# First adaLN chunk of a two-layer decoder trunk in two halves of the channels

## Chip, cores and metric

The kernel runs on one core of a Trainium2 chip. The metric is device microseconds (us) of one execution. Engines are called as the profile calls them: PE (TensorE matmul), PEld (its weight load), DVE (VectorE), ACT (ScalarE), POOL (GpSimd), SP (SyncE, which here only issues loads). A trailing q (SPq) is an engine's sequencer.

## What is computed

Two layers over 256 tokens of 1024 channels, float32. Cut to what the change touches:

```python
c_act = silu(c)
for l in range(2):
    mod = c_act @ w_ada[l] + b_ada[l]                     # 1024 x 6144
    shift1, scale1, gate1, shift2, scale2, gate2 = split(mod, 6)
    h = rmsnorm(x, norm1_g[l]) * (1.0 + scale1) + shift1
    u = h @ w_in[l]                                       # 1024 x 3072
    u_b, u_c, u_h, u_q, u_k, u_v = split(u, 6 blocks of 512)
    y_conv = u_b * conv3(u_c * u_h)
    q, k = rope(rmsnorm(heads(u_q))), rope(rmsnorm(heads(u_k)))
    y_att = causal attention of 8 heads of 64 (q, k, v)
    x = x + gate1 * (concat(rmsnorm(y_conv), rmsnorm(y_att)) @ w_out[l])
    x = x + gate2 * hier_moe(rmsnorm(x, norm2_g[l]) * (1.0 + scale2) + shift2)
```

To have u, every one of the 1024 channels of h is needed; h needs shift1 and scale1 of the same channels, and each value of these sums over all 1024 rows of w_ada.

## The kernel before

**Loads.** SP issues one stream of 1 MB units into `raw`, a ring of ten slots of 128 x 2048 floats: first 8 "a" units (w_ada of layer 0, columns 0 to 2047, that is shift1 and scale1), then 12 "w" units of w_in (each 512 of the 1024 rows by one block of 512 columns, blocks in the order q, k, v, then the three of the convolution), then the chunk of the gates ("G", 8 units), w_out, and so on. An "a" unit k holds, in partition p, row 8p + k of w_ada as one piece of 8 KB; a "w" unit holds pieces of 2 KB. SP waits for a slot to be free (`wait_free`) and goes on in order. x, small parameter rows and the gate biases come by ACT's queue, router weights by POOL's.

**adaLN (lines 1088 to 1112, 442 to 448, 753 to 765).** `ada_acc` multiplies each "a" unit by silu(c), repeated over 32 columns: four matmuls a unit write four strips of 32 rows of PSUM bank 6, 512 columns each. They are float32, and the profile records each as two. `ada_out` (ACT) copies the bank to `mod_rows`, `ada_cols` (PE, four matmuls against `rowsel`) turns the rows into columns, `modulation` (DVE) adds the bias and makes the factor.

**Activations.** PE transposes the normed x into banks 0 to 3 (`transposes`), ACT scales and shifts two channel blocks of 128 a bank into `hf` (`norm_evac`, L470), and DVE splits them into a high and a low part (L783, L784), one part for each bank, four in all. act_ready counts them.

**Weights.** Each w unit is two halves of 1024 columns. ACT copies a half rounded into `whi` (L435), DVE subtracts into `wlo` (L694); both are rings of six halves. A product takes three matmuls (`PASSES`).

**q, k, v (L1178).** Block by block: q over all 8 channel blocks into banks 4 and 5, then k into 0 and 1, then v into 2 and 3; 48 matmuls of 512 columns each, 144 in all. Then `conv_block` 0, 1, 2 (L1190, 96 matmuls of 256 columns each), with the transposes of q and k (L1203) between 1 and 2, for which DVE must have done squares, reduction (L805, L807) and rope (L812 to L828).

Every engine works through its own list in order. In layer 0 ACT has: ada_out, norm_evac of four banks, halves 0 to 5, then halves 6 on between the evacuations. DVE has: modulation, four activation parts, halves 0 to 5, the eight trig products (L795), halves 6 to 11, squares and so on. PE has: three "a" units, transposes of parameter rows (L1152, L1155), three "a" units, transposes of x, two "a" units, ada_cols, then q, k, v.

## Time and profile before

| | us |
|---|---|
| median of 3 runs (lowest, highest) | 659.57 (655.09, 663.69) |
| profiled execution, its own time | 659.15 |
| its span, first to last instruction | 657.4 |
| PE busy, matmuls | 578.3 (88%) |
| DVE busy | 281.8 (43%) |
| ACT busy | 217.5 (33%) |
| moved by DMA | 189.76 MB, mean 289 GB/s |

The profile is of one execution; the runs scatter by about 0.7% round their median. Matmuls are pipelined and their ends modelled, so their starts are the surer reading. The clock column has no record before about 28 us, where it prints 1.00; there durations are read instead.

### The profile page before, as it was taken

What the parts mean: (1) busy time and instruction counts of PE and PEld (TensorE: products, weight loads), DVE (VectorE), ACT (ScalarE), POOL (GpSimd) and SP (SyncE); (2) the same over time, 40 slices, a digit from 0 to 9 for tenths busy, and PEclk for the clock granted to TensorE, in tenths of its full rate; (3) what the DMA queues carried; (4) which work ended last, traced back from release to release, by engine and by line L of the source; (5) the groups of instructions that cost most, each with busy time, mean ns of one, the idle gap of its engine ahead of it and who ended that gap; (6) DMA issues with size and microseconds to landing.
All of it is one profiled execution on the core that took longest, in us unless ns stands there. A gap on an engine that the chain in (4) does not pass through costs nothing.

```text
span 657.4 us, 7967 instructions
## 1 busy us (share of the span) xinstructions
PE 578.3 (88%) x3204; PEld 371.1 (56%) x3204; DVE 281.8 (43%) x483; ACT 217.5 (33%) x376; POOL 13.2 (2%) x63
## 2 busy tenths in 40 slices
PE   2759999869799999999948999986977899999993
PEld 0338899446666644444427899754566664444432
DVE  4065790875256111112277595476236401111233
ACT  2064543541134322322135535254105332322210
POOL 6100000000000000000000000000000000000000
PEclk9959999989898799999998999987977679999998
DMA  8999942790399799999999545195058059999951
GB/s 266 371 390 387 376 171 110 286 413 4 135 420 410 274 378 396 413 412 415 406 386 362 201 168 216 65 415 224 1 227 349 0 186 372 409 414 415 414 220 66
DMA packets 48623, 189.76 MB, mean 289 GB/s; under 512 B 4346, under 2 KB 4426, under 8 KB 40388
## 3 DMA queue, kind: packets, MB, share of 16 engines
q1 hardware_dynamic: 47264, 185.62, 72.3%
q10 hardware_dynamic: 900, 3.23, 1.3%
q0 software_dynamic: 416, 0.32, 0.6%
q8 instruction: 29, 0.48, 0.3%
q14 instruction: 14, 0.11, 0.0%
HBM read 188.10 MB, written 1.05 MB: 288 GB/s over the span
## 4 chain that ended last, share of the span: by engine, by line
PE 79%; DVE 9%; DMA 4%; ACT 4%; issue 1%; SPq 1%; DVEq 0%; ACTq 0%
PE ps L1370 18%; PE ps L1190 11%; PE ps L1178 10%; PE ps L1396 9%; PE ps L1350 6%; PE ps L1281 6%; PE ps L1098 5%; PE ps L1410 4%; DMA raw<-in_w_ada_dram 4%; DVE wlo L694 2%; PE ps L1322 2%; PE ps L1121 2%; PE ps L1436 1%; PE ps L1111 1%; PE ps L1271 1%
## 5 line engine op out<-in xcount | busy, mean ns | idle before, releaser
L694 DVE TENSOR_TENSOR wlo<-raw,whi 128x1024 fp32r<-128x1024 f32 x64 | 74.9, 1220 | 14.4 <-ACT whi L435 14.2
L435 ACT ACTIVATE whi<-raw 128x1024 fp32r<-128x1024 f32 x64 | 64.6, 1061 | 26.3 <-PE ps L1178 10.9
L1098 PE MATMUL ps<-raw,c_rep 128*32 128x512 f32 x384 | 53.5, 696 | 17.2 <-DMA raw<-in_w_ada_dram 17.2
L1370 PE MATMUL ps<-raw,qkT 128*64 128x512 f32 x256 | 61.5, 625 | 1.9 <-ACT work L645 1.9
L1396 PE MATMUL ps<-raw,work 128*64 128x512 f32 x256 | 58.0, 598 | 0.0
L1370 PE MATMUL ps<-raw,cbc 128*64 128x512 f32 x256 | 57.2, 594 | 0.0
L1190 PE MATMUL ps<-act_hi,whi 128*128 128x256 f32 x192 | 54.5, 284 | 0.0
L1190 PE MATMUL ps<-act_hi,wlo 128*128 128x256 f32 x192 | 54.3, 283 | 0.0
L1190 PE MATMUL ps<-act_lo,whi 128*128 128x256 f32 x192 | 54.3, 283 | 0.0
L1045 DVE SCALAR_TENSOR_TENSOR work<-ps,cw,work 128x256 f32<-128x256 f32 x16 | 7.7, 483 | 108.1 <-ACT work L639 108.1
L1034 DVE TENSOR_TENSOR v_sb<-ps,gates 128x512 f32<-128x512 f32 x32 | 22.1, 691 | 67.2 <-PE ps L1396 67.2
L1178 PE MATMUL ps<-whi,act_hi 128*128 128x512 f32 x96 | 38.6, 402 | 8.7 <-DVE wlo L694 7.1
L1098 PEld LDWEIGHTS ps<-raw,c_rep 128*32 128x32 f32 x384 | 11.7, 120 | 48.3 <-issue 33.9
L1370 PEld LDWEIGHTS ps<-raw,qkT 128*64 128x64 f32 x256 | 18.1, 143 | 36.0 <-issue 31.5
L1178 PE MATMUL ps<-wlo,act_hi 128*128 128x512 f32 x96 | 38.2, 397 | 0.0
L1178 PE MATMUL ps<-whi,act_lo 128*128 128x512 f32 x96 | 38.1, 396 | 0.0
L1370 PEld LDWEIGHTS ps<-raw,cbc 128*64 128x64 f32 x256 | 18.0, 137 | 34.8 <-issue 33.7
L629 ACT ACTIVATE whi<-v_sb 128x512 fp32r<-128x512 f32 x32 | 20.0, 630 | 53.5 <-DVE v_sb L1034 45.2
L1350 PE MATMUL ps<-whi,act_hi 128*128 128x256 f32 x128 | 37.0, 320 | 0.3 <-DVE whi L990 0.3
L1190 PEld LDWEIGHTS ps<-act_hi,wlo 128*128 128x128 f32 x192 | 36.8, 192 | 0.1
L1190 PEld LDWEIGHTS ps<-act_hi,whi 128*128 128x128 f32 x192 | 36.8, 192 | 0.1
L1190 PEld LDWEIGHTS ps<-act_lo,whi 128*128 128x128 f32 x192 | 36.8, 192 | 0.0
(207 smaller groups left out, 886.7 us busy)
## 6 DMA issues: line engine op xcount, KB each, us to landing
raw<-in_w_ada_dram SPq DMA_DIRECT2D x48, 1024.0 KB, 9.7
raw<-in_w_gate_dram SPq DMA_DIRECT2D x64, 512.0 KB, 7.3
raw<-in_w_up_dram SPq DMA_DIRECT2D x64, 512.0 KB, 9.4
raw<-in_w_down_dram SPq DMA_DIRECT2D x32, 1024.0 KB, 11.5
raw<-in_w_in_dram SPq DMA_DIRECT2D x24, 1024.0 KB, 14.5
raw<-in_w_out_dram SPq DMA_DIRECT2D x8, 1024.0 KB, 6.1
gates<-in_b_ada_dram ACTq DMA_DIRECT2D x4, 512.0 KB, 6.8
res<-in_x_dram ACTq DMA_DIRECT2D x1, 1024.0 KB, 4.9
```

The costliest lines, as they stand in the source:

```text
L435: act.activation(whi[:, slot(n), :], raw[:, r, (i % 2) * 1024:(i % 2 + 1) * 1024], ACT.Copy).then_inc(hi_done, 1)
L629: act.activation(y_hi[:, cols], y_f[:, cols], ACT.Copy).then_inc(yhi_ready, 1)
L694: dve.tensor_tensor(wlo[:, slot(n), :], raw[:, ring_slot[("w", l, i // 2)], (i % 2) * 1024:(i % 2 + 1) * 1024], whi[:, slot(n), :].bitcast ...
L1034: dve.tensor_tensor(y_f[:, cols], ps[:, 2 + n, :], gates[:, 1, cols], ALU.mult).then_inc(yg_ready, 1)
L1098: ins = pe.matmul(ps[32 * i:32 * i + 32, 6, :], c_rep[:, k, :], raw[:, ring_slot[unit], i * 512:(i + 1) * 512], start=(k == 0), stop=(k == ...
L1178: ins = pe.matmul(ps[:, bank + t, :], acts[pa][:, k, t * P:(t + 1) * P], w[pw][:, kk * 512:(kk + 1) * 512], start=(k == 0 and p == 0), sto ...
L1190: ins = pe.matmul(ps[:, bank + j // 2, (j % 2) * S:(j % 2 + 1) * S], w[pw][:, kk * 512 + j * P:kk * 512 + (j + 1) * P], acts[pa][:, k, :], ...
L1281: ins = pe.matmul(ps[:, 2 * t + n, :], acts[pa][:, k, t * P:(t + 1) * P], w[pw][:, n * 512:(n + 1) * 512], start=(k == 0 and p == 0), stop ...
L1350: ins = pe.matmul(ps[:, bank, j * S:(j + 1) * S], xn[part][:, t, k * P:(k + 1) * P], sel[:, t, 256 * q:256 * (q + 1)], start=(t == 0 and p ...
L1370: ins = pe.matmul(ps[i * SLOTS:(i + 1) * SLOTS, 0, :], hg[p // 2 % 2][:, k, c0:c0 + SLOTS], ws[i][:, :, kk, :], start=(k == 0), stop=(k == ...
L1396: ins = pe.matmul(ps[i * SLOTS:(i + 1) * SLOTS, 2 + n, :], hidT[:, p % 2, kk, i * SLOTS:(i + 1) * SLOTS], ws[i][:, c0:c0 + 512], start=(kk ...
L1410: ins = pe.matmul(ps[:, 4 + 2 * t + n, :], selT[:, 2 * p + t, :], ys[part][:, n * 512:(n + 1) * 512], start=(p == 0 and part == 0), stop=( ...
```

## The change

The first chunk is made in two: A0 gives shift1 and scale1 of channels 0 to 511, A1 those of 512 to 1023. An "a" unit of these holds two rows of w_ada (8p + 2i and 8p + 2i + 1) with 512 + 512 columns of each, in two DMAs of 512 KB in pieces of 2 KB; A0 and A1 have four units each. The stream becomes A0, the first w units of q, k and v (channels 0 to 511), A1, the rest. Turning rows into columns (`first_cols`) still takes four matmuls, each time.

PE now has: two A0 units, transposes of parameter rows, transposes of x, two A0 units, first_cols(0), q on channels 0 to 511, one A1 unit, k on these, two A1 units, v on these, one A1 unit, first_cols(1), then q, k and v on channels 512 to 1023. ACT copies the transposes of channels 512 to 1023 out of PSUM unscaled (so that v can use banks 2 and 3) and scales them in place later. DVE has: first_modulation(0), two activation parts, halves 0 to 5, first_modulation(1), two activation parts, the trig products, halves 6 on. The order q, k, v by halves of the channels holds for both layers, and the evacuations of q, k and v and DVE's halves 12 to 23 are moved accordingly. The lines left out are declarations and renumbered semaphore counts.

```diff
@@ -242,19 +244,26 @@
-        chunks = [("A", 0)]
+        chunks = [("A0", 0), ("A1", 0)]
         for l in range(L):
             chunks += [("G", l), ("M", l)] + ([("A", l + 1)] if l + 1 < L else [])
         chunk_of = {q: i for i, q in enumerate(chunks)}
         steps_before = [sum(2 if kind == "G" else 1 for kind, _ in chunks[:i]) for i in range(len(chunks))]
+        chunk_units = [4 if kind in ("A0", "A1") else KD for kind, _ in chunks]
+        units_before = [sum(chunk_units[:i]) for i in range(len(chunks) + 1)]
+
+        def in_unit(u):
+
+            return (IN_ORDER[u % 3], u // 3) if u < 6 else (IN_ORDER[u // 2], u % 2)
         def slot(n):
             return (n + 1) % RING
-        stream = [("a", 0, k) for k in range(KD)]
+        stream = [("a", 0, k) for k in range(4)] + [("w", 0, u) for u in range(3)]
+        stream += [("a", 1, k) for k in range(4)]
         for l in range(L):
-            stream += [("w", l, u) for u in range(0 if l == 0 else 2, 12)]
+            stream += [("w", l, u) for u in range(3 if l == 0 else 2, 12)]
             stream += [("a", chunk_of[("G", l)], k) for k in range(KD)]
@@ -291,6 +300,13 @@
                     row = ada_v[layer, :, i, :]
+                    if which in ("A0", "A1"):
+                        c0 = 512 * int(which == "A1")
+                        for j in range(2):
+                            sp.dma_start(dst.rearrange("p (j v n) -> p j v n", j=2, v=2)[:, j, :, :],
+                                         ada_v[layer, :, 2 * i + j, 0:2 * D].rearrange("p (v n) -> p v n", v=2)
+                                         [:, :, c0:c0 + 512]).then_inc(raw_full[r], 16)
+                        return
                     if which == "G":
@@ -482,15 +498,28 @@
                 root(0, t)
-            ada_out("A", 0)
-            norm_evac(0, range(4))
+            for bank in (2, 3):
+                act.wait_ge(xT_done, bank + 1)
+                ins = act.activation(hf[:, 2 * bank:2 * bank + 2, :],
+                                     ps[:, bank, :].rearrange("p (j s) -> p j s", j=2), ACT.Copy)
+            ins.then_inc(hf_raw, 1)
+            ada_out("A0", 0)
+            norm_evac(0, range(2))
+            split(0, 0)
+            split(0, 1)
+            split(0, 2)
+            ada_out("A1", 0)
+            act.wait_ge(mod_ready, 2)
+            act.wait_ge(hf_raw, 1)
+            for bank in (2, 3):
+                for j in (2 * bank, 2 * bank + 1):
+                    ins = act.activation(hf[:, j, :], hf[:, j, :], ACT.Identity, scale=mod_t[:, 0, 1, j:j + 1],
+                                         bias=mod_t[:, 0, 0, j:j + 1])
+                ins.then_inc(hf_act, 1)
             for l in range(L):
                 n0 = HALVES * l
                 m = 2 * l
-                if l == 0:
-                    for u in range(3):
-                        split(l, u)
-                else:
+                if l > 0:
                     for t in range(T):
@@ -500,25 +529,25 @@
                 def qk_out(w):
-                    act.wait_ge(unit_used, n0 + 4 * (w + 1))
+                    act.wait_ge(unit_used, n0 + 8 + 2 * w)
                     bank = (4, 0)[w]
                     for t in range(T):
                         ins = act.activation(tokmaj[:, t, w * AW:(w + 1) * AW], ps[:, bank + t, :],
                                              ACT.Copy)
                     ins.then_inc(proj_evac, 1)
-                qk_out(0)
                 split(l, 4)
                 split(l, 5)
+                qk_out(0)
+                split(l, 6)
                 qk_out(1)
-                split(l, 6)
                 split(l, 7)
+                act.wait_ge(unit_used, n0 + 12)
+                act.activation(v_sb[:, :, :], ps[:, 2:4, :], ACT.Copy).then_inc(proj_evac, 1)
+                split(l, 8)
                 act.wait_ge(qk_sum, l + 1)
                 act.activation(stat[:, 4:36], stat[:, 4:36], ACT.Sqrt, scale=1.0 / HD,
                                bias=eps_col).then_inc(qk_root, 1)
-                act.wait_ge(unit_used, n0 + 12)
-                act.activation(v_sb[:, :, :], ps[:, 2:4, :], ACT.Copy).then_inc(proj_evac, 1)
-                split(l, 8)
                 split(l, 9)
@@ -750,6 +781,17 @@
+            def first_modulation(a):
+
+                dve.wait_ge(mod_sum, a + 1)
+                ks = slice(4 * a, 4 * a + 4)
+                dve.tensor_tensor(mod_t[:, 0, :, ks], ps[:, 7, 0:8].rearrange("p (j v) -> p v j", v=2),
+                                  mod_col[:, 0, ks, 0:2].rearrange("p j v -> p v j"), ALU.add).then_inc(mod_read, 1)
+                dve.wait_ge(mod_read, a + 1)
+                dve.scalar_tensor_tensor(out=mod_t[:, 0, 1, ks], in0=mod_t[:, 0, 1, ks], scalar=1.0,
+                                         in1=mod_col[:, 0, ks, 6 * L], op0=ALU.add, op1=ALU.mult
+                                         ).then_inc(mod_ready, 1)
+
             def modulation(kind, l):
@@ -771,20 +813,29 @@
-            modulation("A", 0)
+            def activation_parts(l, banks):
+                for bank in banks:
+                    dve.wait_ge(hf_act, 6 * l + bank + 1)
+                    js = slice(2 * bank, 2 * bank + 2)
+                    link(dve.tensor_copy(act_hi[:, js, :], hf[:, js, :]))
+                    dve.tensor_tensor(act_lo[:, js, :], hf[:, js, :], act_hi[:, js, :].bitcast(F32),
+                                      ALU.subtract).then_inc(act_ready, 1)
+
+            first_modulation(0)
+            activation_parts(0, range(2))
+            for u in range(3):
+                split(0, u)
+            first_modulation(1)
+            activation_parts(0, range(2, 4))
             for l in range(L):
                 n0 = HALVES * l
                 if l > 0:
                     for t in range(T):
                         token_scale(2 * l, t)
-                for bank in range(4):
-                    dve.wait_ge(hf_act, 6 * l + bank + 1)
-                    js = slice(2 * bank, 2 * bank + 2)
-                    link(dve.tensor_copy(act_hi[:, js, :], hf[:, js, :]))
-                    dve.tensor_tensor(act_lo[:, js, :], hf[:, js, :], act_hi[:, js, :].bitcast(F32),
-                                      ALU.subtract).then_inc(act_ready, 1)
-                for i in range(0 if l == 0 else 3, 6):
-                    split_half(l, i)
+                if l > 0:
+                    activation_parts(l, range(4))
+                    for i in range(3, 6):
+                        split_half(l, i)
                 if l == 0:
@@ -799,6 +850,7 @@
                 split(l, 5)
+                split(l, 6)
@@ -806,8 +858,8 @@
                                   AX.X, ALU.add).then_inc(qk_sum, 1)
-                split(l, 6)
                 split(l, 7)
+                split(l, 8)
                 dve.wait_ge(qk_root, l + 1)
@@ -828,8 +880,7 @@
                     dve.wait_ge(rope_done, T * l + t + 1)
-                    split(l, 8 + t)
-                split(l, 10)
+                    split(l, 9 + t)
                 split(l, 11)
@@ -1095,10 +1146,21 @@
                     for i in range(4):
-                        ins = pe.matmul(ps[32 * i:32 * i + 32, 6, :], c_rep[:, k, :],
+                        row = 2 * k + i // 2 if q < 2 else k
+                        ins = pe.matmul(ps[32 * i:32 * i + 32, 6, :], c_rep[:, row, :],
                                         raw[:, ring_slot[unit], i * 512:(i + 1) * 512],
-                                        start=(k == 0), stop=(k == KD - 1), skip_group_check=True)
+                                        start=(k == 0), stop=(k == chunk_units[q] - 1), skip_group_check=True)
                     ins.then_inc(ada_used, 1)
+
+            def first_cols(a):
+
+                pe.wait_ge(mod_evac, a + 1)
+                if a > 0:
+                    pe.wait_ge(mod_read, a)
+                for j in range(4):
+                    ins = pe.matmul(ps[:, 7, 2 * j:2 * j + 2], mod_rows[:, j * P:(j + 1) * P], rowsel2[:, :],
+                                    start=True, stop=True)
+                ins.then_inc(mod_sum, 1)
@@ -1141,7 +1203,7 @@
             pe.wait_ge(crep_ready, 2)
-            ada_acc("A", 0, range(0, 3))
+            ada_acc("A0", 0, range(0, 2))
             pe.wait_ge(const_ready, 2)
@@ -1155,30 +1217,42 @@
             ins.then_inc(lines_T, 1)
-            ada_acc("A", 0, range(3, 6))
             transposes(0)
-            ada_acc("A", 0, range(6, 8))
-            ada_cols("A", 0)
+            ada_acc("A0", 0, range(2, 4))
+            first_cols(0)
             for l in range(L):
                 n0 = HALVES * l
                 if l > 0:
                     transposes(2 * l)
-                for i in range(3):
+                for u in range(6):
+                    i, part = u % 3, u // 3
                     bank = (4, 0, 2)[i]
-                    if i > 0 and l == 0:
-                        pass
-                    for half in range(4):
-                        w = wait_half(l, 4 * i + half)
-                        pe.wait_ge(act_ready, 4 * l + (4 if i else half + 1))
+                    if l == 0 and i == 2 and part == 0:
+                        pe.wait_ge(hf_raw, 1)
+                    elif i == 2 and part == 0:
+                        pe.wait_ge(act_ready, 4 * l + 4)
+                    for half in range(2):
+                        w = wait_half(l, 2 * u + half)
+                        if i == 0:
+                            pe.wait_ge(act_ready, 4 * l + 2 * part + half + 1)
+                        elif i == 1 and part == 0 and half == 0:
+                            pe.wait_ge(act_ready, 4 * l + 2)
                         for kk in range(2):
-                            k = 2 * half + kk
+                            k = 4 * part + 2 * half + kk
                             for t in range(T):
                                 for p, (pa, pw) in enumerate(PASSES):
                                     ins = pe.matmul(ps[:, bank + t, :], acts[pa][:, k, t * P:(t + 1) * P],
                                                     w[pw][:, kk * 512:(kk + 1) * 512],
                                                     start=(k == 0 and p == 0), stop=(k == KD - 1 and p == 2))
                         ins.then_inc(unit_used, 1)
+                    if l == 0 and u == 0:
+                        ada_acc("A1", 0, range(0, 1))
+                    elif l == 0 and u == 1:
+                        ada_acc("A1", 0, range(1, 3))
+                    elif l == 0 and u == 2:
+                        ada_acc("A1", 0, range(3, 4))
+                        first_cols(1)
...
```

## Rows read from the trace of the kernel before

**Rows 1.** Page: PE's busy tenths in 40 slices; split of weights on ACT, mean ns.

```profile
PE   2759999869799999999948999986977899999993
...
L435 ACT ACTIVATE whi<-raw 128x1024 fp32r<-128x1024 f32 x64 | 64.6, 1061 | 26.3 <-PE ps L1178 10.9
```

**Rows 2.** Chain of waits, 0 to 125 us: start us, us, what.

```profile
5.02 27.93 DMA raw<-in_w_ada_dram
...
43.75 35.06 PE ps L1178 x144
...
101.88 1.03 ACT cbc L529
```

**Rows 3.** SP's loads into raw, fourth w_ada unit and third w_in unit: duration ns, start.

```profile
L299 SPq DMA_DIRECT2D raw<-in_w_ada_dram x1: 447/447/447, 2.9 to 2.9; - x1
...
DMA to landing us min/median/max: 19.0/19.0/19.0
...
L302 SPq DMA_DIRECT2D raw<-in_w_in_dram x1: 10356/10356/10356, 19.1 to 19.1; - x1
...
DMA to landing us min/median/max: 21.9/21.9/21.9
```

**Rows 4.** Timeline of PE, 0 to 44 us: start us, us, operation, count, idle before.

```profile
15.07 1.94 PE L1098 MATMUL ps<-raw,c_rep 128*32 128x512 f32 x8 [2.81 <-DMA raw<-in_w_ada_dram]
...
20.97 1.97 PE L1152 MATMUL ps<-ident,cbc 16*128 16x16 f32 x16
...
23.29 3.64 PE L1098 MATMUL ps<-raw,c_rep 128*32 128x512 f32 x16
...
28.63 1.97 PE L1130 MATMUL ps<-ident,tokmaj 128*128 128x128 f32 x16
30.52 1.07 PE L1098 MATMUL ps<-raw,c_rep 128*32 128x512 f32 x8
...
34.77 1.87 PE L1111 MATMUL ps<-rowsel,mod_rows 128*128 128x4 f32 x8 [0.72 <-ACT mod_rows L448]
```

**Rows 5.** Timeline of DVE, 36 to 50 us: modulation, first activation part, six weight splits.

```profile
36.95 0.17 DVE L763 SCALAR_TENSOR_TENSOR mod_t<-mod_t,mod_col 128x8 f32<-128x8 f32 x1
38.22 0.43 DVE L783 CAST act_hi<-work 128x512 fp32r<-128x512 f32 x1 [1.09 <-ACT work L470]
...
42.47 6.89 DVE L694 TENSOR_TENSOR wlo<-raw,whi 128x1024 fp32r<-128x1024 f32 x6
```

**Rows 6.** Chain of waits, later: the same forms at full rate.

```profile
125.80 3.57 PE ps L1098 x32
...
206.06 0.88 PE ps L1111 x8
...
350.80 32.90 PE ps L1178 x144
```

**Rows 7.** Timeline of DVE, 49 to 86 us: trig products to the first rope.

```profile
49.29 1.16 DVE L795 TENSOR_TENSOR trig<-sincos,g_qk 128x64 f32<-128x64 f32 x8
...
69.08 2.48 DVE L805 TENSOR_TENSOR work<-tokmaj 128x1024 f32<-128x1024 f32 x2 [4.18 <-ACT tokmaj L506]
71.60 2.29 DVE L807 TENSOR_REDUCE stat<-work 128x32 f32<-128x2048 f32 x1
...
78.34 0.35 DVE L812 RECIPROCAL stat<-stat 128x32 f32<-128x32 f32 x1
...
83.85 2.36 DVE L694 TENSOR_TENSOR wlo<-raw,whi 128x1024 fp32r<-128x1024 f32 x2
```

**Rows 8.** Windows: us, busy PE, PEld, DVE, ACT, POOL, granted clock, DMA share, GB/s.

```profile
40.00:45.00 5.00, 1.25 (x3) 1.06 (x4) 4.93 (x8) 5.00 (x8) 0.00 (x0) 0.50 1.05 388
...
120.00:125.00 5.00, 2.55 (x23) 1.24 (x16) 4.79 (x9) 3.85 (x17) 0.00 (x0) 1.00 0.99 376
```

**Rows 9.** DMA, 270 to 330 us (expert stage), and landings of loads, 75 to 95 us.

```profile
DMA packets 6132, 24.61 MB, mean 410 GB/s; under 512 B 566, under 2 KB 566, under 8 KB 5009
...
DMA to landing us min/median/max: 4.9/5.9/6.0
```

More of the change, by code:

```diff
@@ L93, in trunk @@
         rowsel = sb("rowsel", [P, 4])
+        rowsel2 = sb("rowsel2", [P, 2])
         mask = sb("mask", [P, 384])
@@ L170, in trunk @@
         xT_done = sem("xT_done")
+        hf_raw = sem("hf_raw")
         hf_act = sem("hf_act")
@@ L276, in trunk @@
             r = pos % RAW
-            counts[r] += 32 if unit[0] == "g" else 16
+            counts[r] += 32 if unit[0] == "g" or unit[0] == "a" and unit[1] < 2 else 16
             ring_slot[unit], landed[unit] = r, counts[r]
@@ L300, in load @@
                 elif kind == "w" and i < 12:
-                    blk, half = IN_ORDER[i // 2], i % 2
+                    blk, half = in_unit(i)
                     sp.dma_start(dst.rearrange("p (k n) -> p k n", k=4),
@@ L321, in wait_free @@
                 if kind == "a":
-                    sp.wait_ge(ada_used, KD * l + i + 1)
+                    sp.wait_ge(ada_used, units_before[l] + i + 1)
                 elif kind == "w":
@@ L444, in ada_out @@
                 q = chunk_of[(kind, l)]
-                act.wait_ge(ada_used, KD * (q + 1))
+                act.wait_ge(ada_used, units_before[q + 1])
                 if q > 0:
@@ L464, in norm_evac @@
             def norm_evac(m, banks):
-                act.wait_ge(mod_ready, m + 1)
+                act.wait_ge(mod_ready, m + 2 if m > 0 else 1)
                 for bank in banks:
@@ L716, in _ @@
             dve.memset(stat[:, 63:64], EPS).then_inc(crep_ready, 1)
+            dve.memset(rowsel2[:, :], 0.0)
             link(dve.memset(rowsel[:, :], 0.0))
             for i in range(4):
+                dve.memset(rowsel2[32 * i:32 * i + 1, i % 2:i % 2 + 1], 1.0)
                 last = dve.memset(rowsel[32 * i:32 * i + 1, i:i + 1], 1.0)
@@ L943, in _ @@
                 dve.reciprocal(stat[:, 1:2], stat[:, 3:4]).then_inc(rstd_ready, 1)
-                dve.wait_ge(mod_ready, m + 1)
+                dve.wait_ge(mod_ready, m + 2)
                 for bank in (2, 3):
@@ L1423, in _ @@
                 if l + 1 < L:
-                    pe.wait_ge(mod_ready, m + 2)
+                    pe.wait_ge(mod_ready, m + 3)
                 pe.wait_ge(over_known, l + 1)
```

## The prediction, made before the changed kernel was timed

> **What bounds the kernel now.** I read the page first, its line of PE's busy tenths: nearly all digits are 7 to 9, but the first two are 2 and 7 [rows 1]. The start is where PE is not yet the bound. The chain of waits says what is instead: 27.93 us of it are one landing of adaLN weights, issued at 5.02 and there at 32.95, and from 43.75 PE works without a gap to 101.9, where an evacuation comes in [rows 2]. The question is therefore how early the q, k, v matmuls (L1178) can end; they end at 43.75 + 35.06 = 78.81, and what follows is a PE chain that starts from there.
>
> Landings next. Issue time plus time to landing gives for the fourth megabyte of the chunk 2.9 + 19.0 = 21.9 us and for the third of w_in, the eleventh in the stream, 19.1 + 21.9 = 41.0 [rows 3]; the eighth has 32.95. That is one megabyte in 2.7 us from the fourth to the eighth, whose pieces have 8 KB, and in 2.7 us from there to the eleventh, whose pieces have 2 KB.
>
> The path between the last landing and the first matmul is read off the timelines. PE accumulates the eighth unit in 1.1 us from 32.95, ACT evacuates, PE turns the rows into columns from 34.77 on [rows 4], and DVE is done with the modulation at 37.12 [rows 5]. ACT and DVE then evacuate and split the activations, four parts of 1.06 us on DVE (38.22 to 42.47), DVE splits the first weights (6.89 / 6 = 1.15 us each) [rows 5], and PE starts at 43.75.
>
> **The start of the first half, costed.** After the change PE needs only four units (4 MB, landed at 21.9). Its queue: unit 1 ends at 17.0 (15.07 + 1.94), the small transposes of the parameter rows take 20.97 to 23.29 = 2.3, transposes(0) 28.63 to 30.52 = 1.9, units 2 and 3 at 1.94 each [rows 4]: 17.0 + 2.3 + 1.9 + 3.9 = 25.1. By then all of it has landed, so PE, not the DMA, ends the first half. ACT's raw evacuation of banks 2 and 3 comes before the new ada_out; it can begin at 21.2 and copies 128x1024 in all, about 1.0 us by L529 [rows 2], done before 25.1, so it costs nothing. From the end of the accumulation to mod_ready was 34.1 to 37.12 = 3.0; first_cols still issues four matmuls (eight records), so it stays 3.0: 28.1. From mod_ready to the first matmul was 6.6; two of the four activation parts (2 x 1.06 = 2.1) leave the path: 4.5. PE starts at **32.6 instead of 43.75: -11.1**. Bounds: with units 2, 3 and the columns at the faster rate that the same forms show later (1.07 a unit at 30.52, 0.88 for the columns at 206 [rows 4, 6]) it is 29.9; if the parameter rows land only at 20.97, which the trace does not exclude, 36.6.
>
> **What comes onto PE.** The A1 units used to be accumulated while PE had nothing else. Now they stand between the q, k and v parts. They have landed by then (32.95 to 41.0, the places of the old eighth to eleventh megabyte), so each costs only its work, 3.57 / 4 = 0.89 us at full rate [rows 6]: **+3.6**. The matmuls themselves keep their number, 144, and their slow beginning: the same 144 take 32.90 in layer 1, at full rate throughout [rows 6], and 35.06 here, 2.2 more. u0, u1, u2 with the four units between them take 16.45 + 2.2 + 3.6 = 22.2 us and end at 54.8.
>
> **The new bubble.** The fourth A1 unit ends at 54.8, almost fourteen us after it landed, and nothing that PE could do stands behind it. In order: evacuation 0.7, columns 0.88 at full rate [rows 6], modulation 0.4: mod_ready at 56.8 (2.0 together). Then ACT scales the first bank, 37.16 to 38.22 = 1.06 before, now out of SBUF; the nearest rows, 128x1024 from SBUF in 1.06 and from PSUM in 1.02, say that the source changes little [rows 1, 2]. DVE splits two activation parts (2.1). And then, ahead of the first wlo of w3, DVE has the eight trig products of L795: in the kernel before they ran at 49.29 for 1.16 us under PE's work [rows 7]; here they stand alone, 1.2. Last one wlo, 1.2. 1.06 + 2.1 + 1.2 + 1.2 = 5.6. ACT's halves 6 and 7 are ready in that time; its two gate bias DMAs are issued by its sequencer while ACT works. **Bubble 2.0 + 5.6 = +7.6**; PE restarts at 62.4.
>
> **The restart.** After the gap of 7.1 us before 43.75 the granted clock was 0.50 (1.2 of 2.4 GHz) [rows 8]. Against it, from 120 to 125 PE was busy for 2.55 of 5 us and kept 1.00 [rows 8]. Here PE has two gaps, 0.7 and 5.6 us, round 0.88 of columns; that is nearer to the first row, so I take the same price again: **+2.2**, bounds 0 and 3. The Trainium skill (TensorE: Matmul & The Clock Gate, HAM oscillation) says that an idle gap puts the array back to half rate and each restart pays anew, which speaks against splitting one long run into two; by it the sum is the one below, without it 2.2 less.
>
> **Sum.** -11.1 + 3.6 + 7.6 + 2.2 = **+2.3 us** at the end of v: 81.1 instead of 78.8.
>
> **What I cost at nothing.** (a) The later q and k. All three blocks now end in the last half of the section, so DVE's squares, reduction and rope start later in both layers: k is out at 77 instead of 69. Squares and reduction take 4.8, a pair of wlo 2.4, one rope 78.34 to 83.85 = 5.5 [rows 7]. A conv block takes 11.5 us (78.81 to 101.88 for two), so its second unit is wanted 5.8 after its start. From k out, DVE has unit 7 ready at 76.7 + 4.8 + 2.4 = 83.9, wanted at 81.1 + 5.8 = 86.9; then unit 8, a rope and unit 9 by 94.2, wanted at 98.4; the second rope (5.1) by 99.3, wanted by the transposes at 105.2. The old slack was about 11 us (the second rope ended some 7.5 after 83.85, the transposes began at 102.9). If the cover were gone, each us of lateness beyond 3 would show in each layer. (b) Sixteen transfers of 512 KB for eight of 1 MB: SP issues one in about 0.45 us [rows 3], and the stream needs 1.35 us for 512 KB. In the expert stage, where gate and up come in transfers of 512 KB, the stream keeps 410 GB/s [rows 9]. (c) The gate biases (1 MB) are loaded 15 us later; they are wanted far behind, by the gates after the attention. (d) SP's ring: w6 to w11 wait for slots that first-half units free earlier than before, and units 8 MB ahead are not on the path. (e) Layer 1: same units in the same number, 32.90 us together, with act_ready asked no earlier than before. (f) The memsets of rowsel2 run on DVE while it waits for positions and x.
>
> **Rivals.** *The change does what it says:* the second half's modulation is hidden, the bubble and the second slow start vanish, and -11.1 + 3.6 = -7.5 remains: 651.6 us. For it: A1 has landed at 41.0. Against it: first_cols(1) follows the last accumulation directly, and the splits of w3 stand behind it on ACT and DVE. An earlier start at 29.9 or no slow restart alone gives 657 to 659. Chance of the whole or most of it 0.08.
>
> *The split transfers come late.* In a quiet queue a 1 MB transfer takes 4.9 us to land [rows 9] against 2.7 in the stream, so 2.2 us of it are fixed. If the four extra DMAs of A0 each paid that, A0 lands at 30.7; unit 3 ends at 32.6, 7.5 us later than I have it, and the time is 669.0. A1 would land at 58.6, still before PE wants its last unit. The stream's rate in the expert stage speaks against it. Chance 0.07. The Trainium skill (DMA: Bandwidth & Descriptors, Bandwidth) asks for at least 1 MiB a DMA and gives one as 2.0 us plus bytes / 436 GB/s; an estimate by that page, were the eight of 512 KB run one after another, is 26 us for A0, and the trace at 410 GB/s does not bear it out.
>
> *Slower, by DVE.* Between k out and the second rope DVE is on the path. It decides when DVE's work there (22 us: squares to second rope) runs more than 3 us later than summed; at 9.6 us late, 6.6 show in each of two layers, and the time is 661.5 + 13.2 = 675. The durations come from rows, so it would need another wait there, such as ACT's square root standing behind v's evacuation. Chance 0.04.
>
> **Numbers.** The forecast has 0.81. Against the profiled execution's own time of 659.15 (span 657.4 plus 1.75) the sum gives 661.5; that execution is 0.4 below the median of the runs. The bounds give 656.6 (PE starts at 29.9 and restarts at full rate, -2.7 and -2.2) to 666.3 (late parameter rows and a restart of 3, +4.8), and the rivals 651.6, 669.0 and 675; with less than two in ten left out, and two or three us for the spread of the runs, the range is 653.5 to 667.5. Two per cent, about what a measurement of this kernel can tell from no change, is 13.2 us: only below 646.4 or above 672.8. Even the first rival in full does not reach that on the fast side. Faster 0.03, within 0.92, slower 0.05.
>
> **What the new profile would show.** First L1178 near 32.6 (not before 30) and A0's last unit done near 25; the first half's q, k, v ending with the fourth A1 unit near 55; a PE gap of about 5.6 us before the second half, its last releaser DVE's wlo, with the trig products just before it; half rate after it; L1190 starting near 81; no wait of L1190 or L1203 on DVE. I am wrong if the second gap is much shorter, if A0 lands after 25, or if PE waits in conv blocks 0 or 1.

## The result, and the profile after

| | before | after |
|---|---|---|
| median (lowest to highest), us | 659.48 (655.09 to 663.69), 4 executions | 669.48 (668.46 to 670.33), 4 executions |
| ratio, 95% interval | | 1.0152 (1.0084 to 1.0220) |
| profiled execution, span | 657.4 | 666.7 |
| its mean granted clock | 0.929 | 0.912 |

The changed kernel is 10 us, 1.5%, slower; the forecast was 661.5, in a range up to 667.5. Ratios in this document leave out executions more than 1.5% above the fastest of their kernel; medians count all.

First the start of the changed kernel. The chain of waits, start us, us, what; L1150 accumulates adaLN units, L1161 makes columns, L1245 is q, k, v, L1264 the conv blocks:

```profile
3.17 12.37 DMA raw<-in_w_ada_dram
...
26.17 1.07 PE ps L1161 x8
...
32.19 8.15 PE ps L1245 x24
40.34 0.99 PE ps L1150 x8
41.34 5.67 PE ps L1245 x24
47.01 1.85 PE ps L1150 x16
48.86 5.71 PE ps L1245 x24
54.57 1.04 PE ps L1150 x8
55.63 0.61 ACT mod_rows L464
...
56.28 1.07 PE ps L1161 x8
...
63.51 18.77 PE ps L1245 x72
82.28 23.05 PE ps L1264 x192
```

The landing that was 27.93 us of the chain [rows 2] is now 12.37, and q starts at 32.19 instead of 43.75. But the first halves of q, k and v with the A1 units between them last until 55.6, the second half starts only at 63.51, and the section ends at 82.28 against 78.81: **+3.5 us** where all of the gain was to be.

The gap from 57.35 to 63.51 is DVE's list, and its timeline shows it whole (start us, us, operation):

```profile
57.57 0.17 DVE L791 SCALAR_TENSOR_TENSOR mod_t<-mod_t,mod_col 128x4 f32<-128x4 f32 x1
58.90 0.43 DVE L820 CAST act_hi<-work 128x512 fp32r<-128x512 f32 x1 [1.16 <-ACT work L516]
59.36 0.69 DVE L821 TENSOR_TENSOR act_lo<-work,act_hi 128x512 fp32r<-128x512 f32 x1
...
61.03 1.17 DVE L846 TENSOR_TENSOR trig<-sincos,g_qk 128x64 f32<-128x64 f32 x8
62.23 6.90 DVE L723 TENSOR_TENSOR wlo<-raw,whi 128x1024 fp32r<-128x1024 f32 x6
```

Modulation, a wait for ACT's scaling, two activation parts, the trig products that had lain under PE's work [rows 7], one weight split.

The section is a third of the loss. The windows, cut at the same instructions in both kernels, tell where the rest is (us of the stretch, busy time and count of PE, PEld, DVE, ACT, POOL, granted clock, DMA share, GB/s). Before:

```profile
104.05:158.62 54.57, 46.60 (x345) 30.39 (x344) 33.75 (x59) 21.81 (x49) 0.00 (x0) 0.94 0.53 212
158.62:345.95 187.33, 172.74 (x880) 95.19 (x881) 59.72 (x117) 54.91 (x99) 0.00 (x0) 0.94 0.90 357
345.95:383.70 37.75, 36.17 (x162) 30.33 (x163) 26.17 (x36) 18.80 (x26) 0.00 (x0) 0.96 0.70 247
408.94:466.84 57.90, 49.93 (x346) 31.22 (x344) 34.41 (x60) 21.93 (x49) 0.00 (x0) 0.88 0.51 200
466.84:657.40 190.56, 169.08 (x808) 98.10 (x808) 52.12 (x103) 49.60 (x92) 0.00 (x0) 0.91 0.67 265
```

After, the same five:

```profile
107.53:165.72 58.19, 50.21 (x345) 32.13 (x344) 34.43 (x60) 21.81 (x49) 0.00 (x0) 0.85 0.53 212
165.72:352.57 186.85, 172.23 (x880) 94.98 (x880) 59.09 (x115) 54.84 (x99) 0.00 (x0) 0.94 0.90 358
352.57:392.31 39.74, 38.56 (x162) 32.04 (x163) 23.40 (x32) 18.90 (x25) 0.00 (x0) 0.89 0.70 249
417.55:476.22 58.67, 50.32 (x345) 32.12 (x344) 34.42 (x60) 21.81 (x49) 0.00 (x0) 0.85 0.52 210
476.22:666.70 190.48, 169.15 (x809) 98.18 (x808) 52.16 (x103) 49.55 (x92) 0.00 (x0) 0.91 0.66 265
```

The same instructions (345, 880, 162), yet the attention of layer 0 takes 58.19 instead of 54.57 us (+3.6), the start of layer 1 39.74 instead of 37.75 (+2.0), layer 1's attention +0.8; the rest is within 0.5. Wherever time was lost the granted clock is lower: 0.85 against 0.94, 0.89 against 0.96, 0.85 against 0.88. It is not longer waiting: in layer 0's attention PE is idle for 7.97 us before and 7.98 after, and all that was lost is in its busy time (50.21 against 46.60). With 3.5 of the section the sum is 3.5 + 3.6 - 0.5 + 2.0 + 0.8 - 0.1 = 9.3, the difference of the spans. So 5.8 us were lost behind the section, at half rate. The attention is code that the change left as it was. In the start of layer 1 the change did alter the order of q, k, v, but that is not what costs the 2.0 us: this stretch took 39.77 in a profile with the old order (e6) and 37.74 in two with the new one (e8, e11). None of my terms covered the 5.8 us.

Inside layer 0's attention the chains show where it happens. Before:

```profile
139.32 1.14 DVE gates L772
140.45 0.14 issue
140.59 3.58 PE ps L1121 x4
...
146.67 3.22 PE ps L1271 x8
...
151.62 7.00 PE ps L1098 x64
```

After:

```profile
142.81 1.14 DVE gates L814
143.95 0.14 issue
144.08 3.75 PE ps L1183 x4
...
150.96 3.78 PE ps L1345 x8
...
157.19 8.53 PE ps L1150 x64
```

In both kernels PE waits 3.7 us for DVE's gates ahead of the first of these matmuls, and in both the granted clock goes to 0.50 towards the end of that wait. Before, it stood there from about 140.4 to 143.9 and again from 147.3 to 150.7; after, from about 143.2 to 160.3 without a break. The wait is the same; what differs is when full rate comes back. The start of layer 1 has the same picture behind a wait of 7.8 us: full rate is back at 348.7, ahead of q, k, v (350.8), in the kernel before, and at 361.6, four us into them, in the changed one.

### The profile page after: what moved, and what is told of

It is laid out like the page before. It is cut to its first block, busy times and chain, and to the rows that moved or that the text cites. A ratio compares the mean times of both kernels' runs of the same rounds, so it can differ in the third digit from the quotient of the medians.

```text
span 666.7 us, 7993 instructions
## 1 busy us (share of the span) xinstructions
PE 586.5 (88%) x3212; PEld 378.5 (57%) x3212; DVE 282.4 (42%) x490; ACT 218.8 (33%) x379; POOL 13.2 (2%) x63
## 4 chain that ended last, share of the span: by engine, by line
PE 81%; DVE 10%; ACT 4%; DMA 2%; issue 1%; DVEq 0%; SPq 0%; ACTq 0%
PE ps L1444 17%; PE ps L1245 11%; PE ps L1264 10%; PE ps L1470 9%; PE ps L1424 6%; PE ps L1355 6%; PE ps L1150 6%; PE ps L1484 4%; DVE wlo L723 2%; DMA raw<-in_w_ada_dram 2%; PE ps L1183 2%; PE ps L1396 2%; PE ps L1192 1%; PE ps L1510 1%; PE ps L1345 1%
## 5 line engine op out<-in xcount | busy, mean ns | idle before, releaser
L1150 PE MATMUL ps<-raw,c_rep 128*32 128x512 f32 x384 | 50.9, 670 | 13.7 <-DMA raw<-in_w_ada_dram 13.7
L1264 PE MATMUL ps<-act_hi,whi 128*128 128x256 f32 x192 | 54.5, 284 | 0.0
L1264 PE MATMUL ps<-act_hi,wlo 128*128 128x256 f32 x192 | 54.3, 283 | 0.0
L1264 PE MATMUL ps<-act_lo,whi 128*128 128x256 f32 x192 | 54.3, 283 | 0.0
L1245 PE MATMUL ps<-whi,act_hi 128*128 128x512 f32 x96 | 40.8, 425 | 12.3 <-DVE wlo L723 11.1
L1245 PE MATMUL ps<-wlo,act_hi 128*128 128x512 f32 x96 | 39.9, 416 | 0.0
L1245 PE MATMUL ps<-whi,act_lo 128*128 128x512 f32 x96 | 39.7, 414 | 0.0
L1264 PEld LDWEIGHTS ps<-act_hi,wlo 128*128 128x128 f32 x192 | 36.8, 192 | 0.1
L1264 PEld LDWEIGHTS ps<-act_hi,whi 128*128 128x128 f32 x192 | 36.8, 192 | 0.1
L1264 PEld LDWEIGHTS ps<-act_lo,whi 128*128 128x128 f32 x192 | 36.8, 192 | 0.0
L1424 PEld LDWEIGHTS ps<-whi,act_hi 128*128 128x128 f32 x128 | 26.4, 206 | 18.2 <-issue 18.2
```

The costliest lines, as they stand in the source:

```text
L1150: ins = pe.matmul(ps[32 * i:32 * i + 32, 6, :], c_rep[:, row, :], raw[:, ring_slot[unit], i * 512:(i + 1) * 512], start=(k == 0), stop=(k ...
L1245: ins = pe.matmul(ps[:, bank + t, :], acts[pa][:, k, t * P:(t + 1) * P], w[pw][:, kk * 512:(kk + 1) * 512], start=(k == 0 and p == 0), sto ...
L1264: ins = pe.matmul(ps[:, bank + j // 2, (j % 2) * S:(j % 2 + 1) * S], w[pw][:, kk * 512 + j * P:kk * 512 + (j + 1) * P], acts[pa][:, k, :], ...
L1424: ins = pe.matmul(ps[:, bank, j * S:(j + 1) * S], xn[part][:, t, k * P:(k + 1) * P], sel[:, t, 256 * q:256 * (q + 1)], start=(t == 0 and p ...
```

## The experiments

The question after the result: do those 5.8 us come anew in each execution by chance (A), do they come with a later schedule (B), or do they depend on where the section ends against the changes of the clock (C)? And are the terms of the section what I said?

**The kernel before again (e1).** No edit.

> The kernel before once more, to see the stretch from 119 us on in a second profiled execution. Theory A (the 5.9 us that the changed kernel loses behind the q, k, v matmuls come from where the stretches of half rate fall, and these fall anew in each execution): the spans scatter by some 5 us and a new profile shows other stretches of half rate than 140.4 to 143.9 and 147.3 to 150.7. Theory B (they come with the schedule): the same stretches again within 1 us, span 655 to 660.

Median 656.84 (654.96 to 659.85) in 10 executions, ratio 0.9988 (0.9953 to 1.0023). The profiled one has span 654.0 and clock 0.936, and layer 1's attention took 53.7 us there against 57.9 in the first profile. So half rate does fall differently from one execution to the next. Layer 0's attention was as before, though (54.65 us, with half rate in the same two stretches), so theory B had this part right. The kernel before has a spread of 9 us: over 31 executions of that chip 654.4, at a clock of 0.936, to 663.4, at 0.921.

**The new order of q, k, v alone (e2).** On the kernel before:

```diff
-                    blk, half = IN_ORDER[i // 2], i % 2
+                    blk, half = in_unit(i)
-                for i in range(3):
+                for u in range(6):
+                    i, part = u % 3, u // 3
```

with the evacuations and DVE's splits moved as in the change.

> The kernel before with one part of the change alone: q, k, v by halves of the channels in both layers, with the evacuations and the splits moved as in the change; the first chunk stays whole. My prediction's point (a) costs this at nothing: 657 to 662 us, the first q, k, v matmul at 43.7, the last ending at 78.8, no wait in the conv blocks. The rival (DVE late behind k) would show a wait of L1190's counterpart or of the transposes of q and k on DVE and 2 us or more in each layer.

Median 659.97 (655.25 to 661.08), ratio 1.0030 (1.0002 to 1.0057). In its chain the conv blocks follow q, k, v without a wait (43.95 + 35.67, then 23.05 us for 192 matmuls as before), and no DVE piece stands between. Point (a) holds: DVE's later work is covered. Layer 0's attention took 56.3 us here and the start of layer 1 39.7, at a lower clock than before; the 0.3% are within what half rate moves.

**Trig products early (e3, again in e15).** On the changed kernel, DVE:

```diff
             for u in range(3):
                 split(0, u)
+            trig_products(0)
             first_modulation(1)
             activation_parts(0, range(2, 4))
```

> The changed kernel with the eight trig products of layer 0 moved ahead of first_modulation(1), into time in which DVE waits. If the gap of 6.2 us before the second half is the chain modulation, scaling, two activation parts, trig products, one weight split, it shrinks by 1.2 to 5.0 us and the last q, k, v matmul ends at 81.1 instead of 82.3. If something else held PE there (ACT's halves 6 and 7), nothing moves. The total follows by 1.2 us, or by more or less if the stretches of half rate fall otherwise.

PE's gap fell from 6.18 to 5.04 us and the second half started at 61.96: the term is right. But the whole kernel came to 660.68 (658.48 to 663.03), ratio 1.0056 (1.0030 to 1.0081): 1.2 us of work moved off the path, some 8 us gained. None of its ten executions had a clock below 0.924.

**A1 behind the first part of q (e4, e8, e16).** On the changed kernel, PE:

```diff
+                        if l == 0 and u == 1 and half == 0:
+                            first_cols(1)
                     if l == 0 and u == 0:
-                        ada_acc("A1", 0, range(0, 1))
-                    elif l == 0 and u == 1:
-                        ada_acc("A1", 0, range(1, 3))
-                    elif l == 0 and u == 2:
-                        ada_acc("A1", 0, range(3, 4))
-                        first_cols(1)
+                        ada_acc("A1", 0, range(0, 4))
```

> The changed kernel with all four A1 units accumulated directly behind the first part of q and first_cols(1) in the middle of the first part of k, so that the second modulation lies under the rest of k and v. If the bubble is an order of work and not a late landing, PE runs without a gap from 32.2 to the end of v: 82.3 - 7.9 (bubble) - 2.3 (half rate after it) + 1.0 (columns) = 73 us, some 6 us ahead of the kernel before; the whole kernel 653 to 661 us. If A1 lands later than the 41 us of my sum, PE waits in the A1 units instead and the end lies later by that wait.

q, k, v started at 33.41 and ended at 73.81 with no gap: the four A1 units took 3.64 us at 41.79, the columns 0.95 at 48.22. So the bubble was the order of PE's list, not a landing, and the whole of it can be hidden. The kernel as a whole: 658.23 (651.73 to 660.50), ratio 0.9991 (0.9954 to 1.0028). Its ten executions fall apart by clock: three at 651.7 to 653.7 with 0.933 to 0.934, four at 658.8 to 660.5 with 0.916, and three at 655.1 to 659.0 between. The 5 us are won in the section and mostly lost again behind it: in the profiled execution (660.41) the two attentions took 58.2 and 58.7 us.

**The changed kernel again (e5, e13).** No edit.

> The changed kernel once more, in many executions. The q, k, v section accounts for +3.5 us. Theory A (the other 5.9 us are half rate that falls anew in each execution): the executions scatter over 5 us or more, as those of the kernel before and of e4 did (654 to 663, 652 to 660), with a median of 657.6 + 3.5 = 661 us. Theory B (the shifted schedule keeps PE at half rate behind it in every execution): again 668 to 670 with a granted clock of 0.909 to 0.912 in all.

668.57 (664.63 to 670.35) in 5 executions, ratio 1.0148 (1.0098 to 1.0199); one had 0.924 and 664.63, four had 0.912. With the first four and e13's five, 13 of 14 executions on several chips lie at 0.909 to 0.912. Theory A falls: chance would not miss so evenly.

The exception is the execution that was profiled here, and it tells more than the rest. Its section ended at 84.61, 2.3 us later than in the first profile, and its two attentions took 54.35 and 54.78 us instead of 58.19 and 58.67, at 0.94 instead of 0.85. With no line of code changed, a later end of the section went with 3.8 us less in all (664.63 against 668.46).

**The kernel before, delayed (e6).** DVE, ahead of the first weight split of layer 0:

```diff
+                if l == 0:
+                    for _ in range(8):
+                        link(dve.memset(trig[:, :, :, :, :], 0.0))
```

> The kernel before with eight fills of an unused tile, each waited for, on DVE ahead of its first weight split: the q, k, v matmuls start about 3.5 us later (3 to 5), nothing else differs, and they end about where those of the changed kernel do. Theory A: the median moves by the delay alone, to some 661 us. Theory B (a shift of that size is enough to bring the half rate behind it): 666 to 670 us.

The fills took 0.66 us each, 5.1 together, more than expected; q, k, v started at 47.90 and ended at 82.44, where the changed kernel's end. The median is 664.48 (659.45 to 668.62) against 659.77, ratio 1.0078 (1.0039 to 1.0116): +4.7 us for a section that ends 3.6 later, between the forecasts of both theories. In the median a shift costs about what it is, and the changed kernel with the same end of the section is 4 us slower; so a shift alone does not bring the whole loss. But it brings part of it: in the profiled execution (665.80) layer 0's attention took 58.27 us and the start of layer 1 39.77, as in the changed kernel, while layer 1's attention took 54.51. So these two losses do not need the changed kernel's code.

**The gap filled (e7).** On the changed kernel, PE, behind first_cols(1):

```diff
+                        for _ in range(12):
+                            pe.matmul(ps[0:32, 6, :], c_rep[:, 0, :], tokmaj[:, 0, 0:512],
+                                      start=True, stop=True)
```

> The changed kernel with twelve further matmuls (32 x 512, float32, results thrown away, into a bank that is free) behind first_cols(1), in the gap before the second half. If the second slow start is the answer to PE's idleness, the 72 matmuls after it take 16.5 instead of 18.8 us and the section ends 2.3 us earlier; if half rate comes there anyway, nothing moves. The twelve should take 5.1 us of the 6.2.

The chain of this kernel:

```profile
57.13 10.42 PE ps L1257 x24
67.54 16.54 PE ps L1245 x72
84.09 23.05 PE ps L1267 x192
```

The twelve took 10.4 us, twice what I gave them (0.87 each: only a group of four, on four strips, is done in 0.89), so the second half started 4.0 us later and the section ended at 84.09. But the half ran in 16.54 us, at a clock of 1.00, instead of 18.77: the second slow start is PE's idleness and costs 2.2, as summed. The kernel as a whole: 667.66 (661.60 to 668.56) in 5 executions, ratio 1.0104 (1.0044 to 1.0164).

**The best of both (e8).** e4 with the trig products of e3.

> The version of e4 (A1 behind the first part of q) with the trig products moved as in e3, where they now cost nothing either way: q, k, v end at 73 to 74 us, as in e4. Under theory A the median is that of e4, 658 us, and over many executions lies below the kernel before; the 5 us gained in the section are shown in full only by the fastest executions (651.7 against 654.4).

654.23 (649.06 to 660.80), ratio 0.9948 (0.9906 to 0.9991), section end 73.22. Again groups: six at 649.1 to 654.2 with 0.926 to 0.938 and five at 658.5 to 660.8 with 0.916.

**The second half later by 0.66, 1.3 and 2.6 us (e9, e10, e11).** On the changed kernel, DVE, ahead of the trig products, with n = 1, 2, 4:

```diff
             activation_parts(0, range(2, 4))
+            for _ in range(n):
+                link(dve.memset(trig[:, :, :, :, :], 0.0))
```

> The changed kernel with one more fill of an unused tile (0.66 us with its wait) on DVE just ahead of the trig products, so that the second half begins 0.66 us later and nothing else changes. In e3 the second half began 1.2 us earlier and the whole kernel came out 8 us faster, with none of ten executions at a granted clock of 0.912, against eight of nine here. Theory C (what is lost behind the section depends on where its end falls against the changes of the granted clock): the time need not follow the delay; it stays within 664 to 670 and the share of executions at 0.912 changes. Theory D (the times add): 668.6 + 0.7 = 669.3.

> As e9 with two fills: the second half 1.3 us later, which is as far the other way as e3 went. Theory C: more work and less time is possible, a median of 662 to 667 with mostly more than 0.92 of the clock. Theory D: 669.9 us.

> As e9 with four fills: the second half 2.6 us later. Theory C: the median leaves the line of theory D, 671.2 us, by 3 us or more, to either side; expected below it, at 664 to 668. Theory D: 671.2 us.

n = 1: 662.63 (662.08 to 665.43), ratio 1.0102 (1.0070 to 1.0133). n = 2: 663.09 (659.83 to 670.67), six executions at 0.925 to 0.929 and four at 0.912 to 0.915. n = 4: 664.18 (663.41 to 668.52), 1.0130 (1.0093 to 1.0167). Theory D, that the times simply add, wanted 669.3, 669.9 and 671.2. Theory C's own range was missed once: n = 1 came out below its 664. Against the changed kernel in e5, on another chip, more work on the path of PE made the kernel faster by 4 to 6 us.

**The best version, delayed (e12).** e8 with two fills ahead of DVE's first weight split.

> The version of e8 with two fills (1.3 us) ahead of DVE's first weight split, so that q, k, v start and end 1.3 us later, at 74.5. e8 had two groups of executions, 649 to 654 us and 658 to 661. Theory C: the shares of the groups change, and the median with them by more than the 1.3 us. Theory D: 654.2 + 1.3 = 655.5 and both groups 1.3 us later.

655.47 (650.58 to 660.59), ratio 0.9958 (0.9921 to 0.9995), section end 73.00 where e8 had 73.22: in this execution the first modulation was 1.0 us earlier (27.25 against 28.22) and the first part of q took 7.35 us instead of 8.18, so the delay of 1.3 does not show at the end. The median is what theory D wanted (655.5) and does not decide for C. One of ten executions at 0.919, none at 0.916: the groups changed, as only C has it. This and e8 are the two that came out ahead of the kernel before, by 0.4 to 0.5%, with intervals that end just short of 1.

**Side by side on one chip (e13 to e16).** The changed kernel, e9, e3 and e8 again.

> The changed kernel beside e14 to e16 on one chip, since e9 ran on another chip than e5. Theory C holds if it is again at 667 to 670, mostly at a granted clock near 0.912, where e14 stays near 663. Theory D: e14 is 0.7 us slower than this.

> e9 again beside the changed kernel on the same chip. Theory C: 662 to 665 us, some 5 us faster than e13 with 0.66 us more work on the path. Theory D, or a difference of chips: 0.7 us slower than e13.

> e3 again on the same chip: 660 to 662 us, by theory C; 1.2 us faster than e13 by theory D.

> e8 again: the section ends 5 us before that of the kernel before. Both groups of executions again (649 to 654, 658 to 661), a median of 653 to 658, 0.5% ahead of the kernel before.

| | section ends | median of all | clocks | ratio (95%) |
|---|---|---|---|---|
| e13, changed kernel | 82.78 | 669.56 | 0.910 to 0.912, all 5 | 1.0180 (1.0128 to 1.0232) |
| e14, second half 0.66 later | 84.08 | 662.83 | 0.924 to 0.927, 3 of 11 at 0.917 | 1.0097 (1.0064 to 1.0130) |
| e15, trig products early | 81.90 | 661.97 | 0.924 to 0.929, all 11 | 1.0060 (1.0026 to 1.0094) |
| e16, A1 early as well | 72.98 | 658.55 | 0.933 to 0.938 (4), 0.916 to 0.921 (7) | 0.9976 (0.9928 to 1.0023) |
| kernel before | | 657.66 | 0.921 to 0.937 | |

It is not the chip. The same windows as above, layer 0's and layer 1's attention, for e13:

```profile
108.03:166.22 58.19, 50.22 (x345) 32.13 (x344) 34.41 (x60) 21.81 (x49) 0.00 (x0) 0.85 0.53 212
418.03:476.73 58.70, 50.36 (x346) 32.15 (x344) 34.43 (x60) 21.80 (x49) 0.00 (x0) 0.85 0.52 211
```

and for e14, which has one fill of 0.66 us more:

```profile
109.33:163.94 54.61, 46.63 (x345) 30.35 (x344) 33.79 (x59) 21.81 (x49) 0.00 (x0) 0.94 0.56 226
416.52:471.14 54.62, 46.64 (x346) 30.40 (x344) 33.79 (x59) 21.82 (x49) 0.00 (x0) 0.94 0.56 226
```

3.6 and 4.1 us in the two attentions, 7.7 together, at 0.85 against 0.94 of the clock. e13's section ended 1.3 us earlier, and the other stages behind it were 1.5 us shorter in e13's profile than in e14's: 7.7 - 1.3 - 1.5 = 4.9 us, the difference of the two spans (667.4 and 662.5). The medians differ by 6.7; the execution profiled in e14 (664.33) lay 1.5 above its median.

All 18 profiles, of twelve different kernels, put in the order in which their section ended:

| section ends | layer 0's attention, us | profiles |
|---|---|---|
| 72.98, 73.00, 73.22 | 53.7, 56.0, 53.7 | e16, e12, e8 |
| 73.81 | 58.2 | e4 |
| 78.52, 78.81 | 54.7, 54.6 | e1, before |
| 79.61 | 56.3 | e2 |
| 81.08, 81.90 | 54.4, 54.5 | e3, e15 |
| 82.28, 82.44, 82.78 | 58.2, 58.3, 58.2 | after, e6, e13 |
| 83.11, 84.08, 84.09 | 53.7, 54.6, 54.6 | e9, e14, e7 |
| 84.19 | 56.3 | e10 |
| 84.61, 86.51 | 54.4, 54.5 | e5, e11 |

The attention has only a few lengths, and neighbours mostly share them whichever kernel they come from: the three that ended between 82.28 and 82.78 are two profiles of the changed kernel and one of the kernel before, delayed. That is what theory C says of this stage; with one or a few profiles at each place it is support and not proof. e16 did not repeat e8's lead: over both, 22 executions, the version with the section 5 us shorter has about as many good executions (649 to 656) as bad ones (658 to 661).

## Why the prediction was wrong, step by step

**The landings** were right. The last of A0 is issued at 5.6 and takes 17.0, so 22.6 us (forecast 21.9), and the last of A1 is issued at 31.1 and takes about 11.4, so 42.5 (forecast 41.0). Eight transfers of 512 KB landed 0.7 us later than four of 1 MB had: the rival of the split transfers is out. The Trainium skill (DMA: Bandwidth & Descriptors, Bandwidth) asks for at least 1 MiB a DMA; this trace, with several loads outstanding all the time, does not show the price of staying below it. The fixed 2.0 us that the prediction cites stands on the same page under another heading (Anatomy of one DMA — SWDGE (gpsimd) path), for DMAs issued by GpSimd; these are issued by SP.

**The first start** was 32.19 for 32.6, and in part by luck. transposes(0) took 3.6 us instead of 1.9, and the two A0 units behind them 2.06 instead of 3.9: each ran at the other rate than in the kernel before, the two misses of 1.7 and 1.8 cancelled, and the accumulation ended at 25.4 for 25.1. The columns took 1.07 us against 1.87 [rows 4], within my bounds. From mod_ready on it was 4.5, as summed.

**A1 on PE** was 0.99 + 1.85 + 1.04 = 3.9 for 3.6, and the three first parts of 24 matmuls took 8.15, 5.67 and 5.71 instead of 7.7, 5.5 and 5.5, 0.9 more together, which no row of mine could show.

**The bubble** was 55.61 to 63.51 = 7.9 for 7.6, in the order that I gave, trig products included; e3 and e4 show that this chain and PE's order make it. **The restart** was 2.3 for 2.2, and e7 shows that it is idleness. The Trainium skill (TensorE: Matmul & The Clock Gate, HAM oscillation) says so, and here the trace agrees.

**The sum of the section** was +3.5 for +2.3: 0.5 less at the start, 0.3 more for A1, 0.9 for the three parts, 0.3 for the bubble and 0.1 for the restart. **The costs at nothing** held in the section: L1264 starts at 82.28, as the last q, k, v matmul ends, and e2 shows no wait on DVE. Point (e) did not: q, k, v of layer 1 took 34.88 us, not 32.90, since their first four us ran at half rate; that is the 2.0 us of the start of layer 1.

**What failed** is the step from the section to the kernel: "the sum gives 661.5" added 2.3 us to an execution and took everything behind 78.8 as a chain that only moves. The chain moved by 3.5 and then lost 5.8 in stages behind the section, since PE was at half rate for longer in them, behind waits as long as before. I had the clock as a price of the gap that I saw, and not as a property of all later gaps, of which the kernel before has several: PE waits 3.7 us for the gates in the attention and 7.8 ahead of layer 1. (The stretch at 120 to 125 that I looked at [rows 8] is the one that kept 1.00.) How much of what follows those waits is at half rate can differ with less than a us between two schedules: 58.2 us of attention with the section's end at 82.78 (e13), 53.7 with it at 83.11 (e9). My two or three us for the spread of the runs was too little for that: the kernel before alone spreads over 9 us with it. The rivals did not have it either; the one on the slow side, DVE, was not at work, and that the kernel is slower at all is no merit of its 0.04.

**What stays open.** That the 5.8 us are half rate, and that 0.66 us more or 1.2 us less ahead of the second half takes most of it away, is shown, on one chip and in profiles of both. That it goes by where the section ends is supported by the table of the 18 profiles, for layer 0's attention. Why the changed kernel falls so evenly into the bad case (13 of 14) where others spread is not shown. It is consistent with the end of the section being set in part by the moment at which full rate comes back, so that the attention always meets the clock's changes at nearly the same place; no run here tests that by itself. Why e8 gave 654 and e16 658.6 is open in the same way, and so is when the clock goes back to full rate behind a wait.

## What to carry to other kernels

Splitting a late input in two pays only if its second half's preparation lies under work that PE already has. Here it had landed 12 us before PE took it up, and placing its accumulation one block earlier (e4) took away 8.5 us of section time; ask of each new hand-over what stands ahead of it in every engine's list, the trig products here. And before a gain or loss of under 1% is believed, compare cuts at the same instructions with their granted clock: where PE has waits in later stages, a shift by one microsecond can move more time than the change itself.

## What the runs showed of the hardware

The time of a kernel is not monotonic in its work. On one chip: 669.6 us, with 0.66 us more 662.8, with 1.2 us less 662.0; the difference is in how long the granted clock is at its lower level (0.5 of 2.4 GHz) in stages that lie 45 to 415 us later. In the two attentions the same 345 matmul records took 54.6 us at a mean of 0.94 and 58.2 to 58.7 at 0.85.

Behind the same wait of 3.7 us the lower level lasted 7 us, in two pieces, in one profile (before) and 17 us without a break in another (after).

A float32 matmul of 128 x 512 on 32 columns costs 0.87 us when issued alone into one strip (e7, 24 records in 10.42 us at a clock of 1.00), and four of them on four strips 0.89 to 0.93 (3.57 us for four such groups, 1.85 for two): the strips run beside each other.
